# A YOCO step on one core: page scores in eight groups of two pages, six key pages ahead, the bias table later, key rows finished by ScalarE

## The chip, the cores and the metric

The kernel runs on one core of one Trainium2 chip. The metric is the device time of one execution in microseconds (us), from runs of the same program on the same chip; fewer is better.

## The reference

One inference step of a hybrid decoder with D = 1024 for 256 prompt tokens and 8 x 8 sample tokens (320 rows). Layer one is retention (4 heads, chunks of 128). Then one shared K/V is made from the residual stream, and layer two is block-sparse attention (8 heads of 128) that reads it. Each of the 8 sample sequences also has 2 pages of 128 old positions in a paged cache. The part that matters here:

```python
kv = rmsnorm(x, kv_norm_w) @ w_kv
k, v = jnp.split(kv, 2, axis=-1)
k = rmsnorm(k.reshape(B, T, MOBA_HEADS, MOBA_HD), k_norm_w)
...
k_past = cache_k[pages].reshape(past, MOBA_HEADS, MOBA_HD)
...
s_own = jnp.einsum('qhd,qlhd->qhl', q, k_own).astype(jnp.float32) + b_own
...
p = jax.nn.softmax(logits, axis=-1)
```

For the sample tokens all 256 old positions and the own ones are scored, with a bias by distance.

## The kernel before

The kernel is written as one program per engine, all of which walk the same list of steps, made by hand in `make_schedule` (L133 to L294). The large work is the projections: weights come in chunks of 1 MB (SyncE, `load_chunk`, L648), ScalarE rounds them to a high part (`w_hi`, L1208), VectorE makes the rest (`w_lo`, L1537), and TensorE (PE) multiplies high by high, high by low and low by high into a PSUM bank per tile (L888, L904, L907, in `project`, L847). A chunk of the key projection (`mk`) has three tiles: two of 12 matmuls, one of 8. Each tile has a place in its middle and one at its end, the gaps, into which `make_schedule` puts other steps. The lists `g` count these gaps: 0 to 5 lie in chunk mk(0,0), 6 to 11 in mk(0,1), 12 to 17 in mk(1,0), 18 to 23 in mk(1,1), 24 to 29 in the first chunk of the value projection. The stage from 331.6 to 405.7 us of the profiled run is these five chunks; "key stage" means it.

The steps in these gaps:

- `KP n`, VectorE: turns page n of old keys (L1829) from a cache slot into `ktc` or a part of `scr` (`ktc2`), 128 x 1024. 16 pages; SyncE loads page n + 3 at KP n, with four DMAs, into one of NCP = 4 slots, once page n - 1 has been turned (`load_page`, L682).
- `KS q`, PE: plain fp32 scores of the sample queries (spread out in `wide`) against four turned pages: 64 matmuls of 32x32 by 256 columns (L1079), each shown as two records. KS 0 and 1 add up in PSUM banks 3 to 6 (`PS_BANKS`), KS 2 and 3 again. KP n waits for the group that read its place before.
- `SE 0` and `SE 1`, VectorE: take these banks out, with the bias (L1842, four operations).
- `KX c`, PE: transposes finished key rows into banks 6 and 7 (L1095); VectorE and ScalarE copy them to `mkT` (L1832, L1469).
- A tile of `mk`: ScalarE squares it (L1376), VectorE sums per head (L1697), ScalarE takes the root (L1378), VectorE the reciprocal (L1700) and then four multiplies of 128x128, each by the row's factor and by `k_norm_w` (`knw`) (L1706), into `rows`. SyncE stores `rows` to the outputs k_out at KX 0 and KX 2 (L812). The first multiply of the second half of the keys waits until the first half has been stored (`rows_stored`).
- At KP 10 SyncE also issues the bias table `tb` of 1 MB (L806). `SN`, `SA`, `SD` and `SB` are the scores against the own rows and the softmax. From L1138 on `PV` multiplies with the pages of old values, which use the same cache slots (pages 16 to 31 in `load_page`).

Within an engine steps run strictly in order, and SyncE's DMA issues too: an issue that waits holds all behind it.

## Time and profile before

| | us |
|---|---|
| median of 3 runs | 518.03 (517.72 to 518.62) |
| the profiled execution | 518.44 |
| its span | 516.7 |
| PE busy in it | 495.1 |
| VectorE busy | 362.6 |
| ScalarE busy | 252.2 |

A row of instructions in the profile gives the line, the engine, the operation, what it writes and reads, how many there are, the busy time and the mean time in ns of one, and then the idle time before them and what ended it. PEld is the load of weights into the array, DVE is VectorE, ACT is ScalarE, SPq is SyncE's queue. PEclk, the granted clock, is 1.00 at 2.4 GHz and 0.50 at 1.2 GHz. "issue" is a wait for nothing that the profile shows. The stages before 331 us are the retention layer and the query projection, those after 405 us the values, the attention and the output.

### The profile page before, as it was taken

The page shows a single profiled execution, that of the slowest core. Times are in us where ns is not written, and L with a number is a line of the kernel's source. Part 1 is how long each engine was busy: PE and PEld are TensorE (multiplying, and loading weights), DVE is VectorE, ACT ScalarE, POOL GpSimd, SP SyncE. Part 2 cuts the span into 40 slices and gives each one's busy share as a digit, 9 for nine tenths or more (in the row PEclk, how much of TensorE's full clock was granted, in tenths as well). Part 3 has the DMA queues.
Part 4 walks back from the last instruction along what each step waited for, and adds up shares of the span by engine and source line. Part 5 has one row for each costly group of instructions (what it writes and reads, how often), then busy time and mean ns, then how long its engine had stood idle before and what let it go on. Part 6 is the DMA issues. An engine that isn't in the chain of part 4 may idle for free.

```text
span 516.7 us, 9892 instructions
## 1 busy us (share of the span) xinstructions
PE 495.1 (96%) x3689; PEld 427.3 (83%) x3689; DVE 362.6 (70%) x655; ACT 252.2 (49%) x508; POOL 87.9 (17%) x123
## 2 busy tenths in 40 slices
PE   8999999999999999999999999996776999999997
PEld 6989977898779977897999999874555878999885
DVE  3865449882989549891898888868647664776662
ACT  6736631773436641672734547733113655555540
POOL 0381005320082004520000144410000000000000
PEclk9999999999999999999999999997978999999999
DMA  9992959999799989999659989369888437785211
GB/s 272 357 348 84 297 224 352 376 330 270 271 358 324 220 239 335 387 284 219 203 168 317 314 218 255 100 206 253 242 209 257 163 121 244 236 308 175 82 51 51
DMA packets 86291, 125.53 MB, mean 243 GB/s; under 512 B 4820, under 2 KB 51109, under 8 KB 86117
## 3 DMA queue, kind: packets, MB, share of 16 engines
q1 hardware_dynamic: 86162, 124.90, 78.2%
q8 instruction: 29, 0.48, 0.4%
q14 instruction: 18, 0.14, 0.1%
q10 hardware_dynamic: 82, 0.02, 0.0%
HBM read 98.93 MB, written 27.57 MB: 245 GB/s over the span
## 4 chain that ended last, share of the span: by engine, by line
PE 69%; DVE 16%; DMA 7%; issue 3%; ACT 2%; SPq 2%; POOL 0%; DVEq 0%; ACTq 0%; POOLq 0%
PE bank L907 34%; PE bank L904 15%; PE bank L888 5%; DVE w_lo L1537 5%; DMA w_raw<-in_ret_w_in 3%; DMA w_raw<-in_ret_w_out 3%; DVE st L1759 3%; PE bank L1079 2%; PE bank L1138 2%; DVE scr L1829 1%; PE bank L1016 1%; DVE ktc L1829 1%; PE bank L1184 1%; DMA v_rows<-vs_split 1%; DVE scr L1795 1%
## 5 line engine op out<-in xcount | busy, mean ns | idle before, releaser
L1537 DVE TENSOR_TENSOR w_lo<-w_raw,w_hi 128x512 fp32r<-128x512 f32 x207 | 144.4, 736 | 63.5 <-ACT w_hi L1208 62.9
L1208 ACT ACTIVATE w_hi<-w_raw 128x512 fp32r<-128x512 f32 x208 | 118.7, 621 | 61.9 <-PE bank L907 33.6
L907 PE MATMUL bank<-xn_hi,w_hi 128*128 128x320 f32 x320 | 100.2, 317 | 0.9 <-ACT w_hi L1208 0.7
L907 PE MATMUL bank<-xn_hi,w_lo 128*128 128x320 f32 x320 | 97.7, 309 | 0.1
L907 PE MATMUL bank<-xn_lo,w_hi 128*128 128x320 f32 x320 | 97.6, 309 | 0.0
L904 PE MATMUL bank<-w_hi,xn_hi 128*128 128x512 f32 x160 | 65.7, 411 | 0.0
L907 PEld LDWEIGHTS bank<-xn_hi,w_hi 128*128 128x128 f32 x320 | 59.7, 188 | 5.3 <-issue 3.6
L904 PE MATMUL bank<-w_hi,xn_lo 128*128 128x512 f32 x160 | 63.0, 394 | 0.0
L904 PE MATMUL bank<-w_lo,xn_hi 128*128 128x512 f32 x160 | 63.0, 394 | 0.0
L907 PE MATMUL bank<-ym_hi,w_hi 128*128 128x320 f32 x192 | 60.9, 317 | 0.0
L907 PEld LDWEIGHTS bank<-xn_lo,w_hi 128*128 128x128 f32 x320 | 59.8, 188 | 0.4 <-DVE xn_lo L1586 0.2
L907 PEld LDWEIGHTS bank<-xn_hi,w_lo 128*128 128x128 f32 x320 | 59.7, 188 | 0.3 <-DVE w_lo L1537 0.3
L907 PE MATMUL bank<-ym_hi,w_lo 128*128 128x320 f32 x192 | 59.3, 309 | 0.0
L907 PE MATMUL bank<-ym_lo,w_hi 128*128 128x320 f32 x192 | 59.3, 309 | 0.0
L1759 DVE SCALAR_TENSOR_TENSOR st<-st,bank 128x512 f32<-128x512 f32 x64 | 39.6, 682 | 5.2 <-PE bank L1030 5.2
L904 PEld LDWEIGHTS bank<-w_hi,xn_hi 128*128 128x128 f32 x160 | 30.5, 191 | 9.7 <-issue 3.7
L907 PEld LDWEIGHTS bank<-ym_hi,w_hi 128*128 128x128 f32 x192 | 36.1, 188 | 1.8 <-issue 1.7
L907 PEld LDWEIGHTS bank<-ym_lo,w_hi 128*128 128x128 f32 x192 | 36.1, 188 | 0.1
L1969 POOL TENSOR_TENSOR fin<-raw_qk,cst 128x320 f32<-128x320 f32 x16 | 17.4, 1108 | 109.9 <-DMA out_ret_state_prompt<-fin 68.7
L904 PEld LDWEIGHTS bank<-w_lo,xn_hi 128*128 128x128 f32 x160 | 30.5, 190 | 6.8
L907 PEld LDWEIGHTS bank<-ym_hi,w_lo 128*128 128x128 f32 x192 | 36.0, 188 | 0.0
L904 PEld LDWEIGHTS bank<-w_hi,xn_lo 128*128 128x128 f32 x160 | 30.7, 192 | 5.6
(280 smaller groups left out, 776.6 us busy)
## 6 DMA issues: line engine op xcount, KB each, us to landing
w_raw<-in_ret_w_in SPq DMA_DIRECT2D x23, 1024.0 KB, 10.8
st<-in_state_ret SPq DMA_DIRECT2D x32, 512.0 KB, 8.9
out_ret_state_sample<-st SPq DMA_DIRECT2D x32, 512.0 KB, 4.6
w_raw<-in_ret_w_out SPq DMA_DIRECT2D x8, 1024.0 KB, 8.7
w_raw<-in_moba_w_in SPq DMA_DIRECT2D x8, 1024.0 KB, 6.5
cache<-in_cache_k SPq DMA_DIRECT2D x64, 128.0 KB, 4.6
w_raw<-in_w_kv SPq DMA_DIRECT2D x8, 1024.0 KB, 7.7
cache<-in_cache_v SPq DMA_DIRECT2D x16, 512.0 KB, 4.4
```

The source lines that it names most:

```text
L888: mm = pe.matmul(bank[b][:, :], xn_hi[:, k, TP:T + TS], w[:, wk, :], start=k == 0 and n == 0, stop=k == KT - 1 and n == 1)
L904: mm = pe.matmul(bank[b][0:m, :], x[:, k, c0:c0 + m], w[:, wk, :], **flags)
L907: mm = pe.matmul(bank[out][:, 0:T], w[:, wk, P * tile:P * tile + P], x[:, k, :], **flags)
L1016: mm = pe.matmul(bank[5][32 * j:32 * j + 32, :], qz[:, q0:q0 + 32], st[:, b, DV * d:DV * d + DV], start=False, stop=g == 1 and d == 1, ski ...
L1079: last[g] = pe.matmul(bank[PS_BANKS[g]][c0:c0 + 32, 0:PAST], wide[rows_at, 8 * h + 2 * e + q // 2, at:at + 32], keys_of, start=q % 2 == 0 ...
L1138: mm = pe.matmul(bank[7][32 * j:32 * j + 32, P * u:P * u + P], window(8 * half_at + 4 * (j // 2) + 2 * pg + j % 2, b % 4), cache[:, (16 + ...
L1184: pe.matmul(bank[6][:, 0:TP], mvp[:, 0, P * h:P * h + P], pt[:, h % 2, 0:TP], start=True, stop=False)
L1208: act.activation(w_hi[:, c % 2, part], w_raw[:, c % RAW, part], ACT.Copy).then_inc(w_hi_done, 1)
L1537: dve.tensor_tensor(w_lo[:, c % 2, part], w_raw[:, c % RAW, part], w_hi[:, c % 2, part].bitcast(F32), ALU.subtract).then_inc(w_lo_done, 1)
L1759: dve.scalar_tensor_tensor(state, state, math.exp(NEW * LOG_DECAY[h]), bank[up_bank(b, d)][:, :], ALU.mult, ALU.add).then_inc(bank_read[up ...
L1829: dve.transpose(keys_turned(n), cache[:, n % NCP, :].rearrange("p (c x j) -> p x c j", c=4, j=32)).then_inc(kt_done, 1)
L1969: done(pool.tensor_tensor(to, x, tab, ALU.mult))
```

## The change

Four edits:

1. **Groups of two pages.** KS has eight groups u of two pages instead of four of four, each of 64 matmuls of 32x32 by 128 columns; the total of columns stays. Groups 0 to 3 fill the banks, then 4 to 7. They stand at gaps 4, 7, 10, 13, 17, 19, 22 and 25, and the transposes of pages 2u+4 and 2u+5 one gap behind group u. KP 0 and 1 move into the last two tiles of the query projection, KP 2 and 3 to gaps 0 and 1. Pages are taken in another order, so that `ktc` and `ktc2` each hold one page of a pair. SE 0 moves from gap 12 to 14, SE 1 from 24 to 26, KX 0 from 14 to 15; KX 1, 2 and 3 stay at 16, 26 and 27.
2. **Six pages ahead.** Pages 4 and 5 go to `early_pages`, the still unused memory of `mkT`, so SyncE loads page n + 5 at KP n. The copies to `mkT` wait until these pages are turned. The residual is kept in cache slots 2, 3 and 0.
3. **The bias table** is issued by SyncE at group 6, behind value pages 1 and 2, instead of at KP 10.
4. **Key rows.** VectorE multiplies the whole tile by `knw` in one operation (new L1734) and takes the reciprocal; a new step `KN` on ScalarE scales the four heads (new L1497), at gaps 8, 10, 12, 20, 22 and 24. Its semaphore `rows_done` is what the stores of k_out and KX wait for.

```diff
@@ -47,7 +47,7 @@
 CW = 2048
 RAW = 3
 NST = 8
-NCP = 4
+NCP, NSLOT = 4, 6
 FAR = PAST + NEW - 1
 LINE = 392
 TOK = [(0, P), (P, P), (TP, TS)]
@@ -111,8 +111,18 @@
 
 def key_page(n):
 
-    q, s, pg = n // 4, n % 4 // 2, n % 2
+    q, pg, s = n // 4, n // 2 % 2, n % 2
     return NPG * (4 * (q // 2) + 2 * s + q % 2) + pg
+
+
+def page_slot(n):
+
+    return n if n < NSLOT else (n - 2) % NCP
+
+
+def page_count(n):
+
+    return sum(64 if m < 16 else 16 for m in range(n + 1) if page_slot(m) == page_slot(n))
 
 
 def sb_bank(pair):
@@ -248,14 +260,18 @@
     g[0].append(("ME", 7))
     g[3] += [("QS", 1), ("QR",)]
     g[5].append(("QT",))
-    for n, at in enumerate((0, 1, 2, 3, 6, 7, 8, 9, 12, 13, 14, 15, 18, 19, 20, 21)):
-        g[at].append(("KP", n))
-    for q, at in enumerate((5, 11, 17, 23)):
-        g[at].append(("KS", q))
-    g[12].append(("SE", 0))
-    g[24].append(("SE", 1))
-    g[14].append(("KX", 0))
+    g[0].append(("KP", 2))
+    g[1].append(("KP", 3))
+    for u, at in enumerate((4, 7, 10, 13, 17, 19, 22, 25)):
+        g[at].append(("KS", u))
+        if u < 6:
+            g[at + 1] += [("KP", 2 * u + 4), ("KP", 2 * u + 5)]
+    g[14].append(("SE", 0))
+    g[26].append(("SE", 1))
+    g[15].append(("KX", 0))
     g[16].append(("KX", 1))
+    for n, at in enumerate((8, 10, 12, 20, 22, 24)):
+        g[at].append(("KN", n))
     g[26].append(("KX", 2))
     g[27].append(("KX", 3))
     g[28] += [("SN",), ("SA", 0), ("SA", 1)]
@@ -536,16 +554,20 @@
 
         def keys_turned(n):
 
-            at = ktc if n % 4 < 2 else ktc2
-            return at[:, n % 2, :, :]
+            return (ktc, ktc2)[n % 2][:, n // 2 % 2, :, :]
+
+        def page_at(n):
...
@@ -682,19 +704,20 @@
             def load_page(n):
 
                 m, vals = (n - 16, True) if n >= 16 else (key_page(n), False)
-                if n >= 16 + NCP:
-                    sp.wait_ge(pv_done, n - 15 - NCP)
-                elif n >= NCP:
-                    sp.wait_ge(kt_done, n - NCP + 1)
+                before = n - (NCP if n >= NCP + NSLOT else NSLOT)
+                if before >= 16:
+                    sp.wait_ge(pv_done, before - 15)
+                elif before >= 0:
+                    sp.wait_ge(kt_done, before + 1)
                 page = sp.value_load(pages[0:1, m:m + 1], min_val=0, max_val=a["cache_k"].shape[0] - 1)
                 if vals:
-                    sp.dma_start(cache[:, n % NCP, :], a["cache_v"][bass.ds(page, 1)].rearrange("o p h d -> p (o h d)"))\
-                        .then_inc(cache_loaded[n % NCP], 16)
+                    sp.dma_start(page_at(n), a["cache_v"][bass.ds(page, 1)].rearrange("o p h d -> p (o h d)"))\
+                        .then_inc(cache_loaded[page_slot(n)], 16)
                     return
                 src = a["cache_k"][bass.ds(page, 1)].rearrange("o (c i) h d -> i (o c) (h d)", i=32)
                 for g in range(4):
-                    sp.dma_start(cache[32 * g:32 * g + 32, n % NCP, :].rearrange("p (c x) -> p c x", c=4), src[:, :, 256 * g:256 * g + 256])\
-                        .then_inc(cache_loaded[n % NCP], 16)
+                    sp.dma_start(page_at(n)[32 * g:32 * g + 32, :].rearrange("p (c x) -> p c x", c=4), src[:, :, 256 * g:256 * g + 256])\
+                        .then_inc(cache_loaded[page_slot(n)], 16)
 
             to, src = chunk_view(w_raw, 0, 0), chunk_source(0)
             sp.dma_start(st[:, 0, :], x_rows[0]).then_inc(x_loaded[0], 16)
@@ -783,13 +806,14 @@
                 elif kind == "US":
                     store_pair(4 * step[1] + 3)
                     load_pair(4 * step[1] + 6)
-                elif kind == "ME" and 1 <= step[1] <= NCP:
+                elif kind == "ME" and 1 <= step[1] <= NSLOT and step[1] != 5:
                     if step[1] == 1:
                         sp.wait_ge(pages_loaded, 16)
                         await_ret_over(sp)
                         sp.dma_start(knw[:, :], bass.AP(a["k_norm_w"].tensor, 0, [[0, P], [1, HD]])).then_inc(knw_loaded, 16)
                     load_page(step[1] - 1)
                 elif kind == "ME" and step[1] == 5:
+                    load_page(4)
                     sp.wait_ge(lines_stored, 64)
                     for h in range(MH):
                         for s in range(2):
@@ -799,16 +823,16 @@
                                 .then_inc(bias_loaded, 16)
                 elif kind == "KP":
                     n = step[1]
-                    if n:
-                        load_page(n + 3)
-                    if n == 10:
-                        await_full(sp, 5, "QSS")
-                        sp.dma_start(tb[:, :, :], bass.AP(scratch.tensor, FAR - P, [[skew, P], [LINE, MH], [1, TP]]))\
-                            .then_inc(tb_loaded, 16)
+                    if 1 <= n <= 13:
+                        load_page(n + NSLOT - 1)
+                elif kind == "KS" and step[1] == 6:
+                    await_full(sp, 5, "QSS")
+                    sp.dma_start(tb[:, :, :], bass.AP(scratch.tensor, FAR - P, [[skew, P], [LINE, MH], [1, TP]]))\
+                        .then_inc(tb_loaded, 16)
                 elif kind == "KX" and step[1] % 2 == 0:
                     p = step[1] // 2
                     for t, (c0, m) in enumerate(TOK):
-                        await_read(sp, *tile_use("mk", 3 * p + t))
+                        sp.wait_ge(rows_done, 3 * p + t + 1)
                         sp.dma_start(k_out[t][:, 512 * p:512 * p + 512], rows[0:m, t, :]).then_inc(rows_stored, 16)
                 elif kind == "SN":
                     load_page(16 + NCP - 1)
@@ -1062,12 +1086,13 @@
                         mm = pe.transpose(bank[7][:, P * t:P * t + P], q_rows[:, P * t:P * t + P], ident)
                     close(mm, 7)
                 elif kind == "KS":
-                    q = step[1]
-                    pe.wait_ge(kt_done, 4 * q + 4)
+                    u = step[1]
+                    q, pg = u // 2, u % 2
+                    pe.wait_ge(kt_done, 2 * u + 2)
                     pe.wait_ge(wide_filled, MH)
-                    if q % 2 == 0:
+                    if u % 4 == 0:
                         for b in PS_BANKS:
-                            await_free(pe, b, "PS", q // 2)
+                            await_free(pe, b, "PS", u // 4)
                     last = {}
                     for e in range(4):
                         for s in range(2):
@@ -1075,19 +1100,19 @@
                             for h in range(2):
                                 for g in range(4):
                                     rows_at, c0 = slice(32 * g, 32 * g + 32), 32 * (2 * h + s)
-                                    keys_of = (ktc, ktc2)[s][rows_at, :, 4 * h + e, :]
-                                    last[g] = pe.matmul(bank[PS_BANKS[g]][c0:c0 + 32, 0:PAST], wide[rows_at, 8 * h + 2 * e + q // 2, at:at + 32],
-                                                        keys_of, start=q % 2 == 0 and e == 0, stop=q % 2 == 1 and e == 3,
+                                    keys_of = (ktc, ktc2)[s][rows_at, pg, 4 * h + e, :]
+                                    last[g] = pe.matmul(bank[PS_BANKS[g]][c0:c0 + 32, P * pg:P * pg + P],
+                                                        wide[rows_at, 8 * h + 2 * e + q // 2, at:at + 32], keys_of,
+                                                        start=u % 4 == 0 and e == 0, stop=u % 4 == 3 and e == 3,
                                                         skip_group_check=True)
-                    if q % 2:
+                    if u % 4 == 3:
                         for g in range(4):
                             close(last[g], PS_BANKS[g])
                     else:
                         last[3].then_inc(ks_done, 1)
                 elif kind == "KX":
                     c = step[1]
-                    for t in range(3):
-                        await_read(pe, *tile_use("mk", 3 * (c // 2) + t))
+                    pe.wait_ge(rows_done, 3 * (c // 2) + 3)
                     def key_columns(i, t):
 
                         c0 = TOK[t][0]
@@ -1464,7 +1489,16 @@
                     ins = act.activation(rsq[:, 16:20], bank[7][:, TP:TP + P].rearrange("p (j m) -> p j m", m=32)[:, :, 0],
                                          ACT.Sqrt, bias=eps[:, 1:2])
                     ins.then_inc(bank_read[7], 1)
+                elif kind == "KN":
+                    n = step[1]
+                    m = TOK[n % 3][1]
+                    await_read(act, *tile_use("mk", n))
+                    for d in range(4):
+                        ins = act.activation(rows[0:m, n % 3, P * d:P * d + P], rows[0:m, n % 3, P * d:P * d + P], ACT.Copy,
+                                             scale=kss[0:m, n % 2, d:d + 1])
+                    ins.then_inc(rows_done, 1)
                 elif kind == "KX":
+                    act.wait_ge(kt_done, NSLOT)
                     await_full(act, 7, *step)
                     act.activation(mkT[:, 2 * step[1] + 1, :], bank[7][:, 0:T], ACT.Copy).then_inc(bank_read[7], 1)
                 elif kind == "SA":
@@ -1687,25 +1721,22 @@
                         m = TOK[i][1]
                         if nk == 0:
                             dve.wait_ge(knw_loaded, 16)
-                        src = bank[b]
                         if i == 2:
-                            src = rows[:, i, :]
                             upper_half(rows[0:TS, i, :], b).then_inc(sum_done, 1)
                         dve.wait_ge(key_sq_done, nk + 1)
                         if nk >= 2:
-                            await_read(dve, *tile_use("mk", nk - 2))
+                            dve.wait_ge(rows_done, nk - 1)
                         dve.tensor_reduce(kss[0:m, nk % 2, :], key_sq[0:m, :].rearrange("p (h d) -> p h d", d=HD), AX.X, ALU.add)\
                             .then_inc(key_sum_done, 1)
-                        dve.wait_ge(kss_done, nk + 1)
-                        done(dve.reciprocal(kss[0:m, nk % 2, :], kss[0:m, nk % 2, :]))
-                        done.wait()
                         if h:
                             dve.wait_ge(rows_stored, 48)
                             await_full(dve, 7, "KX", 1)
-                        for d in range(4):
-                            ins = dve.scalar_tensor_tensor(rows[0:m, i, P * d:P * d + P], src[0:m, P * d:P * d + P],
-                                                           kss[0:m, nk % 2, d:d + 1], knw[0:m, :], ALU.mult, ALU.mult)
-                        ins.then_inc(bank_read[b], 1)
+                        done(dve.tensor_tensor(rows[0:m, i, :].rearrange("p (h d) -> p h d", d=HD),
+                                               (rows[0:m, i, :] if i == 2 else bank[b][:, :]).rearrange("p (h d) -> p h d", d=HD),
+                                               knw[0:m, :].rearrange("p (o d) -> p o d", o=1).broadcast_to((m, 4, HD)), ALU.mult))
+                        done.wait()
+                        dve.wait_ge(kss_done, nk + 1)
+                        dve.reciprocal(kss[0:m, nk % 2, :], kss[0:m, nk % 2, :]).then_inc(bank_read[b], 1)
                         nk += 1
                     elif what == "mo" and i == 2:
                         await_read(dve, xr_bank(4 + h), "XR", 4 + h)
@@ -1823,10 +1854,10 @@
                     done.wait()
                 elif kind == "KP":
                     n = step[1]
-                    dve.wait_ge(cache_loaded[n % NCP], page_loaded(n))
+                    await_page(dve, n)
                     if n >= 4:
-                        await_ks(dve, n // 4 - 1)
-                    dve.transpose(keys_turned(n), cache[:, n % NCP, :].rearrange("p (c x j) -> p x c j", c=4, j=32)).then_inc(kt_done, 1)
+                        await_ks(dve, n // 2 - 2)
+                    dve.transpose(keys_turned(n), page_at(n).rearrange("p (c x j) -> p x c j", c=4, j=32)).then_inc(kt_done, 1)
                 elif kind == "KX":
                     await_full(dve, 6, *step)
                     dve.tensor_copy(mkT[:, 2 * step[1], :], bank[6][:, 0:T]).then_inc(bank_read[6], 1)
```

VectorE around SE 0, before. `scr` and `ktc` are what the transposes (L1829) write; L1842 is SE 0.

```order
L1537 TENSOR_TENSOR w_lo<-w_raw,w_hi 128x512 [waits w_hi_done] x2
L1829 STREAM_TRANSPOSE ktc<-cache 128x1024 [waits bank_full6,cache_loaded0]
L1842 SCALAR_TENSOR_TENSOR ps<-bank,small,bs 128x256 [waits bank_full5,bank_full4,bank_full6,bank_full3,bias_loaded]
L1842 SCALAR_TENSOR_TENSOR ps<-bank,small,bs 128x256
L1842 SCALAR_TENSOR_TENSOR ps<-bank,small,ps 128x256 [waits bank_read5,bank_read3]
...
L1829 STREAM_TRANSPOSE ktc<-cache 128x1024 [waits bank_full6,cache_loaded1]
L1537 TENSOR_TENSOR w_lo<-w_raw,w_hi 128x512 [waits w_hi_done]
L1829 STREAM_TRANSPOSE scr<-cache 128x1024 [waits bank_full6,cache_loaded2]
L1832 COPY mkT<-bank 128x320 [waits bank_full6]
```

The same place after the change, where L1860 is the transpose, L1873 SE 0, L1571 the `w_lo` split and L1863 the copy of KX:

```order
L1571 TENSOR_TENSOR w_lo<-w_raw,w_hi 128x512 [waits w_hi_done] x3
L1860 STREAM_TRANSPOSE ktc<-cache 128x1024 [waits bank_full6,cache_loaded0]
L1860 STREAM_TRANSPOSE scr<-cache 128x1024 [waits bank_full6,cache_loaded1]
L1873 SCALAR_TENSOR_TENSOR ps<-bank,small,bs 128x256 [waits bank_full5,bank_full4,bank_full6,bank_full3,bias_loaded]
L1873 SCALAR_TENSOR_TENSOR ps<-bank,small,bs 128x256
L1873 SCALAR_TENSOR_TENSOR ps<-bank,small,ps 128x256 [waits bank_read5,bank_read3]
...
L1863 COPY mkT<-bank 128x320 [waits bank_full6]
```

Two transposes (KP 10 and 11) and three splits now stand ahead of SE 0, where one transpose and two splits stood, and no transpose is left between SE 0 and the copy.

SyncE at the stores of the first half of the keys, before (L806 is the bias table, L689 and L696 the next page of keys):

```order
L806 DMA tb<-bias_lines 128x8x256 [waits bank_full5]
L812 DMA out_k_prompt<-rows 128x512 [waits bank_read2]
L812 DMA out_k_prompt<-rows 128x512 [waits bank_read0]
L812 DMA out_k_sample<-rows 64x512 [waits bank_read1]
L689 TENSOR_LOAD pages [waits kt_done]
```

and after (L712 and L714 load a page of values, L677 a weight chunk, L836 are the stores, L830 the table):

```order
L712 TENSOR_LOAD pages [waits kt_done]
L712 ISA x2
L714 ISA
L714 DMA cache<-in_cache_v 128x1024
L836 DMA out_k_prompt<-rows 128x512 [waits rows_done] x2
L836 DMA out_k_sample<-rows 64x512 [waits rows_done]
L677 DMA w_raw<-in_w_kv 128x4x512 [waits w_lo_done]
...
L830 DMA tb<-bias_lines 128x8x256 [waits bank_full5]
```

The stores now stand behind the first page of values, whose load waits until page 12 of the keys has been turned (KP 12, gap 18), and the table is behind both.

## Rows read from the trace of the kernel before

**Rows 1.** The page: busy time of each engine, and PE in 40 slices.

```profile
PE 495.1 (96%) x3689; PEld 427.3 (83%) x3689; DVE 362.6 (70%) x655; ACT 252.2 (49%) x508; POOL 87.9 (17%) x123
...
PE   8999999999999999999999999996776999999997
```

**Rows 2.** Windows: length, busy of PE, PEld, DVE, ACT, POOL, PEclk, DMA share, GB/s.

```profile
320.00:330.00 10.00, 10.00 (x73) 9.39 (x72) 9.25 (x18) 8.79 (x23) 3.91 (x12) 1.00 0.35 116
...
350.00:360.00 10.00, 5.04 (x132) 2.84 (x130) 8.50 (x19) 3.90 (x8) 0.00 (x0) 0.68 1.12 234
...
370.00:380.00 10.00, 5.42 (x104) 3.42 (x101) 2.38 (x3) 0.33 (x1) 0.00 (x0) 0.71 1.04 308
380.00:390.00 10.00, 6.66 (x28) 5.13 (x26) 6.40 (x15) 3.32 (x7) 0.00 (x0) 0.95 0.71 167
390.00:400.00 10.00, 8.46 (x149) 6.27 (x150) 8.11 (x18) 2.60 (x6) 1.04 (x2) 0.83 0.87 276
```

**Rows 3.** Waits of PE in the key stage, 331 to 406 us.

```profile
PE bank L1079 <- DVE scr L1829: 9.8, 2, 5.0
PE bank L1079 <- issue: 4.6, 1, 4.6
```

**Rows 4.** The same windows view for three groups of scores, L1079 alone.

```profile
340.30:343.00 2.70, 2.70 (x128) 1.79 (x128) 1.00 0.78 205
355.50:360.00 4.50, 4.50 (x128) 2.66 (x128) 0.50 1.10 257
391.50:395.60 4.10, 4.06 (x128) 2.61 (x128) 0.62 0.94 297
```

**Rows 5.** Chain of waits, 320 to 410 us: start, us, what.

```profile
377.59 4.56 PE bank L904 x12
```

**Rows 6.** Timeline of PE before the first key transposes (L1095).

```profile
363.70 0.39 PE L904 MATMUL bank<-w_hi,xn_hi 128*128 128x512 f32 x1
...
364.39 0.38 PE L1095 MATMUL bank<-eye,rows 128*128 128x128 f32 x2
```

**Rows 7.** Timeline of VectorE between score groups 0 and 1.

```profile
353.15 1.13 DVE L1706 SCALAR_TENSOR_TENSOR rows<-bank,small,knw 128x128 f32<-128x128 f32 x4
354.19 1.24 DVE L1829 STREAM_TRANSPOSE scr<-cache 128x1024 f32<-128x1024 f32 x1
```

**Rows 8.** Groups of VectorE instructions, 331 to 406 us.

```profile
L1829 DVE STREAM_TRANSPOSE scr<-cache 128x1024 f32<-128x1024 f32 x8 | 9.8, 1230 | 0.0
L1563 DVE TENSOR_TENSOR rows<-bank,rows 64x512 f32<-64x512 f32 x2 | 1.3, 672 | 0.0
L1842 DVE SCALAR_TENSOR_TENSOR ps<-bank,small,ps 128x256 f32<-128x256 f32 x2 | 0.9, 480 | 0.1
L1537 DVE TENSOR_TENSOR w_lo<-w_raw,w_hi 128x512 fp32r<-128x512 f32 x20 | 13.1, 674 | 2.0 <-ACT w_hi L1208 2.0
```

**Rows 9.** Forms of L1115, then L1138 (ns min/median/max, first and last start); group 0's.

```profile
L1115 PE MATMUL bank<-mkT,mvp x64: 219/219/243, 403.5 to 404.4; 128*32 128x64 f32 x64
...
L1138 PE MATMUL bank<-cache,wide x256: 272/273/298, 415.7 to 474.4; 128*32 128x128 f32 x128
...
L1079 PE MATMUL bank<-scr,wide 32*32 32x256 f32 x64 | 2.6, 385 | 0.0
```

**Rows 10.** Timeline of SyncE's issues around the bias table.

```profile
367.54 0.42 SPq L806 DMA_DIRECT2D tb<-bias_lines  x1
368.02 1.14 SPq L812 DMA_DIRECT2D out_k_prompt<-rows  x2
369.20 0.74 SPq L812 DMA_DIRECT2D out_k_sample<-rows  x1
```

**Rows 11.** Groups of ScalarE instructions, 331 to 406 us.

```profile
L1269 ACT ACTIVATE tb<-ps 128x256 f32<-128x256 f32 x1 | 0.4, 401 | 0.0
```

**Rows 12.** Issues from 364 to 378 us: KB each, median us to landing.

```profile
tb<-bias_lines SPq DMA_DIRECT2D x1, 1024.0 KB, 6.8
...
out_k_sample<-rows SPq DMA_DIRECT2D x1, 128.0 KB, 8.3
```

34 lines of the change are left out of this document (20 added, 14 removed), and 2 rows, old and new, of the table banks.

## The prediction

> **What bounds the kernel now.** First the page: TensorE (PE) is busy 495.1 us, 96% of the span, and apart from the last slice the digits under 8 stand in slices 28 to 31 alone [rows 1], 349 to 400 us at 12.9 us a slice. So all but some 20 us of this kernel is PE work, and a change pays only in that stage. The windows say which stage: PE is busy 5.04, 5.42, 6.66 and 8.46 of 10 us in four of the windows from 350 us on, at a granted clock of 0.68, 0.71, 0.95 and 0.83; from 320 to 330 us it is full [rows 2]. That is the key projection with the page scores in it. Then its waits: 9.8 us in two waits of the score matmuls (L1079) on VectorE's transposes (L1829), and 4.6 us once on "issue" [rows 3]. The windows of the score groups give the clock's part: the first group takes 2.70 us at 1.00 (2.4 GHz), the two behind the waits 4.50 us at 0.50 (1.2 GHz) and 4.10 us at 0.62 [rows 4]. Last the chain: behind the "issue" wait, 12 projection matmuls take 4.56 us [rows 5]. At full clock three of them start in 0.69 us [rows 6], so 12 take 2.76. The stage loses 9.8 + 4.6 us in waits, 1.8 + 1.4 us of slow score groups and 1.8 us of slow projection.
>
> **Why PE waits there.** VectorE can turn pages 4 to 7 only when group 0 has read pages 0 to 3, and it does so between the pieces of two key tiles: the last transpose starts at 354.19 us, behind a reduce, a reciprocal and 1.13 us of multiplies [rows 7]. Group 1 needs all four.
>
> **The change, part by part.** The sum goes by the profiled run, 518.44 us.
>
> 1. *Groups of two pages, the transposes of group u+2 right behind group u.* A group now needs pages that were due a whole group earlier: between u and u+2 lie 5 or 6 half tiles, each 6 x 0.23 = 1.38 us or 0.9 us, against 2 x 1.23 us of transposes [rows 8]. Both waits go: -9.8 us, and the slow clock behind them: -3.2 us. The first transposes move into the query projection, where VectorE is busy 9.25 of 10 us but PE is never idle [rows 2]; I cost that at nothing, since its cover is weights split well ahead; without it, it is 2.5 us.
>
> 2. *Eight groups of 64 matmuls of 128 columns for four of 64 of 256.* No row shows this form. Before, 4 x 2.7 = 10.8 us at full clock. Upper end: the time of an instruction stays, 8 x 2.70 = 21.6, +10.8 us. Lower end: time goes with columns, 1.35 us a group, no change in all (a gain is excluded: the same columns pass). The nearest rows: 64 records of a 64-column form start within 0.9 us, about 15 ns apart, and the 128-column form lasts 273 ns where the scores' last 385 [rows 9]; records of the scores stand 2.70/128 = 21 ns apart [rows 4]. In these rows time falls with columns, so I take 1.4 us a group, 11.2 us: +0.4 us. The Trainium skill ("TensorEngine Tiling (Array Packing)", Instruction Overhead) gives each matmul an overhead of some 60 cycles, and says that fewer columns than that bring nothing; by it the 128 columns still pay, and an estimate from the page for 64 instructions at 25 ns is 1.6 us a group, +2 us in all. The same page (Key Properties) says that a change of tiling mode drains the engine, which would count against twice as many groups; in the rows PE goes into the first group without idle time [rows 4].
>
> 3. *A new wait at the first key transposes (KX 0).* They write bank 6, which SE 0 must have read, and the bank is complete only with group 3. Before, two gaps and 4.4 us lay between group 1's end and KX 0 (360.0 [rows 4] to 364.39 [rows 6]). Now group 3 stands at gap 13, KX 0 at gap 15: 2 x 1.38 = 2.8 us of PE work. VectorE has to do two transposes (2.4) and SE 0 (1.8: four of 0.45 to 0.48 [rows 8]) first, 4.2 us and some 0.3 us to start: a wait of 1.7 us, and of 3.7 us if the three weight splits ahead of them (0.67 each [rows 8]) have not been done. For KX 2, behind group 7 at gap 25 with one half tile between: 1.8 + 0.3 - 1.4 = 0.7 us, or 2.7 us with the splits. Together 2.4 to 6.4; I take +4 us, near the middle, because the splits follow the weights' arrival.
>
> 4. *k_out behind the first V page.* SyncE must wait for transpose 12 before it issues V page 0, and the three k_out stores are queued behind that; the last lands 8.3 us after issue [rows 12]. Before, they were issued at 368.0 to 369.9 us [rows 10], early. VectorE's first multiply of the second half of the keys waits for them. Transpose 12 ends some 1.4 us after group 4, the stores have landed some 10 us later (0.4 + 1.1 + 0.7 us of issuing [rows 10], then 8.3), and VectorE would be ready 5 us after group 4 (0.9 + 2.8 of PE, 1.3 of square and reduce): it stands some 6 us. Behind it are transposes 14, 15, two tiles, splits and SE 1. PE has 10.9 us of projection and two groups until group 7, so most of it is covered; what is left is 0 to 3.5 us at group 7 and KX 2. I take +2 us.
>
> 5. *Keys: one multiply and four ScalarE steps.* VectorE saves 1.13 us for one operation of about 0.68 us (the 64x512 row of L1563 [rows 8]), 6 times, 2.7 us in all, off PE's path but for part 3, where it is in. ScalarE gets 24 activations of 128x128, each at most the 0.40 us of 128x256 [rows 11], under 10 us, and is idle 6 of 10 us there [rows 2]: nothing. KX needs them, but they are issued one to three gaps ahead.
>
> 6. *The bias table later, six pages ahead.* The 1 MB issued at 367.54 us, just ahead of the "issue" stall [rows 10], moves behind group 6, and two pages come into the stretch from 320 us, where the DMA share is 0.35 [rows 2]. Its first reader stands four gaps into the next chunk but one, over 10 us later, and the landing takes 6.8 us [rows 12]. Nothing on the path by itself. Whether the stall goes with it is a rival: PE's stream now holds 256 more matmuls, and the stall (4.6 + 1.8 us) stays in my forecast once.
>
> 7. *The clock behind the new waits.* 6 us of new waits stand for 9.8 of old ones, which cost 3.2 us of slow clock; in proportion +2 us.
>
> Sum: 518.44 - 9.8 - 3.2 + 0.4 + 4 + 2 + 2 = 513.8. The median of before is 0.4 us under its profiled run: **513.4 us**.
>
> **The rivals.**
> - *The stall goes too.* For: the DMA engines stood at a share of 1.04 in that window, just after the table and the k_out stores were issued, and the stall is one of a kind. Against: more instructions in the same time. 513.4 - 4.6 - 1.8 = 507.0. Chance 0.17.
> - *Small matmuls cost what the big ones did.* Against: rows 9. +10.4: 523.8, slower. It decides from 2.1 us a group on (519.1). Chance 0.06.
> - *A second instruction stall, the slower side.* The stream of PE in the groups is twice as long, in a stretch in which the DMA shares are 0.7 to 1.1 [rows 2]; one more stall of the same price, 6.4 us with its clock, gives 519.8. It decides from 5.7 us on, that is with one whole stall. Chance 0.13.
> - *The new waits take the old ones' place.* Parts 3 and 4 at their upper ends, 6.4 + 3.5, and the whole 3.2 us of clock: 518.4 - 9.8 + 0.4 + 9.9 = 518.9, less 0.4: 518.5, no change. It needs weights that arrive late. Chance 0.13.
> - *Pages late.* The shares were near 1 where the pages were fetched [rows 2]; in a shorter stage the DMA engines may set the pace. 1 to 6 us over the forecast. Chance 0.04.
>
> The forecast itself has 0.47. About 0.2% is what a measurement of this kernel can tell, 517.0 to 519.1. Faster: 0.45 of the forecast, 0.17 and 0.11 of the rest, 0.73. Same 0.10, slower 0.17. The range reaches down to 506.5, which holds the first rival and the lower ends of parts 2 to 4, and up to 519.5, so that the fourth is in, and the second and about half of the third are out.
>
> **What would show it.** No wait of the score matmuls on L1860 (the new number of the transposes) over 0.5 us; groups of 1.1 to 1.6 us; PE waits of 1 to 4 us at the key transposes with VectorE's SE or ScalarE's rows named; VectorE standing some 6 us before the fourth multiply of keys; one "issue" stall. Wrong it is if the groups last over 2 us, if "issue" has over 6 us in the stage, or if PE still waits over 9 us there in all.

## The result and the profile after

| | before | after |
|---|---|---|
| median of 4 runs, us | 518.21 (517.72 to 518.62) | 524.79 (523.28 to 526.29) |
| the profiled execution, us | 518.44 | 526.29 |
| its span | 516.7 | 524.5 |
| PE busy | 495.1 | 500.4 |

The change makes the kernel slower: the ratio is 1.0126, with a 95% interval of 1.0099 to 1.0154. The forecast was 513.4 us, faster with a chance of 0.73; the measured time lies above the range, which ends at 519.5. The profiled run of the changed kernel is the slowest of its four, so a second profile of the same kernel (run e14 below, there the fastest of four) stands beside it where the two differ.

The key stage (the same five chunks) now runs from 331.7 to 413.6 us, 81.9 us for 74.1 before. The page of the kernel after, PE and clock in 40 slices, to hold against [rows 1]:

```profile
PE 500.4 (95%) x4201; PEld 433.0 (83%) x4201; DVE 360.0 (69%) x637; ACT 259.3 (49%) x532; POOL 87.7 (17%) x123
...
PE   8999999999999999999999999996487999999997
...
PEclk9999999999999999999999999999689899999999
```

Waits of PE in the kernel after, 300 to 425 us (engine, line, what ended them: us in total, times, longest). They answer to [rows 3]; L1104 are the scores, L1120 is KX, L1873 is SE.

```profile
PE bank L1120 <- DVE ps L1873: 10.6, 1, 10.6
PE bank L1120 <- DVE scr L1873: 3.6, 1, 3.6
PE bank L1104 <- issue: 3.3, 3, 2.7
```

The two waits of 5 us on the transposes are gone, as meant. In their place PE stands 10.6 us at KX 0 and 3.6 us at KX 2, both times until VectorE has taken the scores out of bank 6. Windows of the kernel after, of the score matmuls alone (columns as in [rows 4]):

```profile
339.16:341.00 1.84, 1.84 (x128) 1.52 (x128) 1.00 0.90 347
...
351.74:353.57 1.83, 1.83 (x128) 1.53 (x128) 1.00 0.04 9
...
398.93:400.76 1.83, 1.83 (x128) 1.52 (x128) 1.00 1.04 320
```

A group of 128 columns takes 1.83 us at full clock, and does so whether the DMA engines are idle (0.04) or full (1.04). Half the columns cost 68% of the 2.70 us in [rows 4], not half.

What held SE 0 is read upwards. Timelines of VectorE, ScalarE and SyncE in the kernel after, each with its engine (in brackets the idle time before and what ended it):

```profile
365.84 1.29 DVE L1571 TENSOR_TENSOR w_lo<-w_raw,w_hi 128x512 fp32r<-128x512 f32 x2 [4.29 <-ACT w_hi L1233]
368.05 0.69 DVE L1571 TENSOR_TENSOR w_lo<-w_raw,w_hi 128x512 fp32r<-128x512 f32 x1 [0.92 <-ACT w_hi L1233]
368.66 1.24 DVE L1860 STREAM_TRANSPOSE ktc<-cache 128x1024 f32<-128x1024 f32 x1
369.82 1.20 DVE L1860 STREAM_TRANSPOSE scr<-cache 128x1024 f32<-128x1024 f32 x1
370.95 0.83 DVE L1873 SCALAR_TENSOR_TENSOR ps<-bank,small,bs 128x256 f32<-128x256 f32 x2
```

```profile
365.18 1.15 ACT L1233 ACTIVATE w_hi<-w_raw 128x512 fp32r<-128x512 f32 x2 [6.38 <-DMA w_raw<-in_w_kv]
```

```profile
336.84 0.40 SPq L677 DMA_DIRECT2D w_raw<-in_w_kv  x1
338.03 17.53 SPq L719 DMA_DIRECT2D cache<-in_cache_k  x16
355.66 0.40 SPq L677 DMA_DIRECT2D w_raw<-in_w_kv  x1
356.84 8.87 SPq L719 DMA_DIRECT2D cache<-in_cache_k  x12
```

Ahead of SE 0 stand the splits of the weights of mk(1,1), those wait for ScalarE, and ScalarE stood 6.38 us for the chunk itself, which SyncE issued at 355.66 us, behind four pages that took it from 338.03 on. The chain of waits names the rest: page 10, the last of the four, waits for its slot until the transpose of page 6 at 350.70, and only then is the chunk issued.

```profile
350.70 1.25 DVE ktc L1860
...
355.66 9.49 DMA w_raw<-in_w_kv
365.18 1.15 ACT w_hi L1233 x2
```

In the kernel before, the same chunk was issued at 344.12 us, 11.5 us earlier, and landed 5.6 us later:

```profile
344.12 0.40 SPq L655 DMA_DIRECT2D w_raw<-in_w_kv  x1
```

The step KP n loads page n + 5, but from page 10 on there are only four slots: page 10 is asked for at gap 5 and can be issued only after the transpose at gap 8, while the chunk's load comes at gap 6, behind it.

KX 2 has a second wait behind it: VectorE's first multiply of the second half of the keys stood 2.7 us for the k_out stores (4.4 us in e14), which now come behind value page 0.

```profile
DVE rows L1734 <- DMA out_k_sample<-rows: 2.7, 1, 2.7
```

**The ledger** of the two profiled runs, which are 7.85 us apart: the waits on transposes -9.8; KX 0 and KX 2 +14.2; issue -1.3 (4.6 to 3.3); eight groups for four at full clock, 14.7 for 10.8, +3.9. The slow clock costs what it did, in other places: in the chain of the kernel after, KX 0 takes 1.51 us where KX 1 takes 0.68, four matmuls behind it 1.71 where four take 0.92 later, 12 matmuls from 382.5 us on some 4.5 for 2.76, and 1.7 us around KX 2 (6 matmuls 2.51 for 1.38); about 5 us in all, for 3.2 + 1.8 before. That is +7.0; some 0.8 us remain that I have put nowhere.

### The profile page after: what moved, and what is told of

It reads as the page before. It is cut to its first block, busy times and chain, and to the rows that moved or that the text cites. A ratio compares the mean times of both kernels' runs of the same rounds, so it can differ in the third digit from the quotient of the medians.

```text
span 524.5 us, 10931 instructions
## 1 busy us (share of the span) xinstructions
PE 500.4 (95%) x4201; PEld 433.0 (83%) x4201; DVE 360.0 (69%) x637; ACT 259.3 (49%) x532; POOL 87.7 (17%) x123
## 4 chain that ended last, share of the span: by engine, by line
PE 77%; DMA 9%; DVE 6%; ACT 3%; issue 3%; SPq 1%; POOL 0%; DVEq 0%; ACTq 0%; POOLq 0%
PE bank L931 39%; PE bank L928 16%; PE bank L912 6%; DMA w_raw<-in_w_kv 4%; DMA w_raw<-in_ret_w_out 3%; PE bank L1040 2%; PE bank L1163 2%; ACT w_hi L1233 1%; PE bank L1054 1%; DVE w_lo L1571 1%; DVE ktc L1860 1%; DMA v_rows<-vs_split 1%; PE bank L987 1%; DMA out_k_sample<-rows 1%; PE bank L1209 1%
## 5 line engine op out<-in xcount | busy, mean ns | idle before, releaser
L1571 DVE TENSOR_TENSOR w_lo<-w_raw,w_hi 128x512 fp32r<-128x512 f32 x207 | 144.6, 737 | 73.1 <-ACT w_hi L1233 72.3
```

The lines of the kernel that those rows point to most:

```text
L1571: dve.tensor_tensor(w_lo[:, c % 2, part], w_raw[:, c % RAW, part], w_hi[:, c % 2, part].bitcast(F32), ALU.subtract).then_inc(w_lo_done, 1)
```

## The experiments

Each is against the kernel before, timed beside it, whose medians were 518.0 to 518.5 us (a single 519.17 beside e13). The single runs of the kernel before lie between 514.7 and 522.2 us, so differences of about 1 us between two experiments mean nothing. Waits come from one profiled run each, and e14 shows how far two profiles of one kernel can differ.

**e1: pages in time.** From the changed kernel:

```diff
-                    if 1 <= n <= 13:
-                        load_page(n + NSLOT - 1)
+                    if 1 <= n <= 4:
+                        load_page(n + NSLOT - 1)
+                    elif n >= 7:
+                        load_page(n + NCP - 1)
```

> The changed kernel, but SyncE issues key page 10 and the later pages only at KP n-3, when their slot is free or nearly so, instead of at KP n-5; pages 4 to 9 as in the change. Theory W (weights held back: SyncE stands for a slot with page 10, and the weight chunk of mk(1,1) queued behind it is issued at 355.66 us and lands at 365.18, so the splits ahead of SE 0 and with them KX 0 wait 10.6 us): the chunk is issued by 348 us, the wait at KX 0 falls to under 3.5 us, the slow clock behind it goes, the k_out stores come before the first value page, and the time is 512 to 517 us. Rival V (VectorE's row of two transposes, three splits and SE 0 is itself the wait): KX 0 still waits 5 us or more, time 519 to 523. Rival G (the eight groups are the loss): over 521 whatever the weights do.

Measured: 519.0 us, ratio 1.0022 (0.9986 to 1.0057): the loss against before is gone, though the time is above the 512 to 517 expected. ScalarE waits 1.49 us, for an earlier chunk, and no longer for this one (issued at 349.88). The edit moves a second thing: value page 0 is now loaded behind the k_out stores, and VectorE no longer waits for them. Waits of PE in e1:

```profile
PE bank L1106 <- issue: 4.4, 3, 3.2
PE bank L1122 <- DVE ps L1875: 4.2, 1, 4.2
PE bank L1122 <- DVE scr L1875: 1.5, 1, 1.5
```

W and V are both true in part: of the wait at KX 0, 4.2 us are VectorE's own row, and what was above that was the late chunk. The time fell by the chunk and the stores together; e2 and e3 take them apart.

**e2: weights first.** From the changed kernel; the stores stay where they are.

```diff
+EARLY = {4: ("mk", 0, 1), 8: ("mk", 1, 0), 11: ("mk", 1, 1)}
...
-                    load_chunk(c + 2)
+                    if chunks[c] not in EARLY.values():
+                        load_chunk(c + 2)
...
+                    if n in EARLY:
+                        load_chunk(chunks.index(EARLY[n]) + 2)
                     if 1 <= n <= 13:
                         load_page(n + NSLOT - 1)
```

> The changed kernel with nothing moved but three weight chunks of w_kv on SyncE: each is issued just ahead of the page that would wait for its slot (pages 9, 13 and 16). The k_out stores stay behind the first value page. W: nearly all of the gain of the run before it, 513 to 518 us, with a wait of up to 3 us of VectorE's L1734 for the stores left. If the stores behind the value page are what costs: 521 us or more. Rival V: 519 to 523 with 5 us or more at KX 0.

Measured: 525.56 us, ratio 1.0129 (1.0056 to 1.0202), a miss. The chunk was issued at 341.92 us and KX 0 waited 4.2 us, the same as in e1, so the mechanism holds; but PE stood 8.1 us on issue. Waits of PE in e2:

```profile
PE bank L1108 <- issue: 8.1, 3, 5.4
PE bank L1124 <- DVE ps L1877: 4.2, 1, 4.2
PE bank L1124 <- DVE scr L1877: 2.9, 1, 2.9
```

So no run shows the early chunk alone to save time: what was won at KX 0 was lost in waits on issue. That wait had been one row of my forecast; e4, e5, e10, e13 and e15 look at it.

**e3: stores first.** From the changed kernel: page 16 is loaded behind the k_out stores of KX 0 and not at KP 11.

```diff
-                    if 1 <= n <= 13:
+                    if 1 <= n <= 13 and n != 11:
                         load_page(n + NSLOT - 1)
...
                         sp.dma_start(k_out[t][:, 512 * p:512 * p + 512], rows[0:m, t, :]).then_inc(rows_stored, 16)
+                    if p == 0:
+                        load_page(16)
```

> The changed kernel with nothing moved but the first value page on SyncE, from ahead of the k_out stores to behind them; the weight chunks stay late. W: VectorE's 2.7 us wait for the stores goes, PE's 10.6 us at KX 0 stay, time 522 to 525 us. If the stores are the main loss: under 520 us.

Measured: 522.17 us, ratio 1.0079 (1.0044 to 1.0113), within the expectation. VectorE's wait for the stores, 2.7 us in the profile after, is gone. But KX 0 waited only 4.9 us, though this edit lies behind it: the chunk was issued at 352.68 us there. So part of the 10.6 us belonged to the one profiled run; see e14. Waits of PE in e3:

```profile
PE bank L1106 <- issue: 6.5, 4, 4.6
PE bank L1122 <- DVE ps L1875: 4.9, 1, 4.9
PE bank L1122 <- DVE scr L1875: 1.0, 1, 1.0
```

The wait at KX 2 is 1.0 us, where the change has 3.6 and 4.5. Over all variants it follows VectorE's wait for the stores: 1.0 to 1.7 us at KX 2 where VectorE waits for none (e1, e3, e9), 2.9 where it waits 1.4 and 2.2 us (e2, e15), 3.6 and 4.5 where it waits 2.7 and 4.4. So the stores behind the value page did cost PE some 2 to 3.5 us at KX 2; e3's time does not show it, because its waits on issue are 3 to 5 us longer than those of the two profiles of the change.

**e4: the late table alone.** From the kernel before: the issue of `tb` moves from KP 10 to KS 3.

```diff
-                    if n == 10:
-                        await_full(sp, 5, "QSS")
-                        sp.dma_start(tb[:, :, :], bass.AP(scratch.tensor, FAR - P, [[skew, P], [LINE, MH], [1, TP]]))\
-                            .then_inc(tb_loaded, 16)
+                elif kind == "KS" and step[1] == 3:
+                    await_full(sp, 5, "QSS")
+                    sp.dma_start(tb[:, :, :], bass.AP(scratch.tensor, FAR - P, [[skew, P], [LINE, MH], [1, TP]]))\
+                        .then_inc(tb_loaded, 16)
```

> The kernel before with one part of the change alone: the 1 MB bias table is issued at KS 3 instead of KP 10. If the table's transfer starved PE of instructions, the 4.6 us of issue in KS 2 and the slow clock behind it go: 512 to 515 us. If it did not (the changed kernel has a stall of 2.7 us in the scores with no table near): 517 to 519 us and a stall of 2 us or more in one of the groups.

Measured: 514.65 us, ratio 0.9932 (0.9907 to 0.9957). The wait at the same place fell from 4.58 us [rows 3] to 1.8; the transposes' 9.8 stayed. Waits of PE in e4:

```profile
PE bank L1079 <- DVE scr L1829: 9.8, 2, 5.0
PE bank L1079 <- issue: 1.8, 1, 1.8
```

**e5: the groups split, alone.** From the kernel before: each group of four pages becomes two halves, back to back.

```diff
+                    for pg, e in [(pg, e) for pg in range(2) for e in range(4)]:
...
-                                    keys_of = (ktc, ktc2)[s][rows_at, :, 4 * h + e, :]
-                                    last[g] = pe.matmul(bank[PS_BANKS[g]][c0:c0 + 32, 0:PAST], wide[rows_at, 8 * h + 2 * e + q // 2, at:at + 32],
+                                    keys_of = (ktc, ktc2)[s][rows_at, pg, 4 * h + e, :]
+                                    last[g] = pe.matmul(bank[PS_BANKS[g]][c0:c0 + 32, P * pg:P * pg + P],
+                                                        wide[rows_at, 8 * h + 2 * e + q // 2, at:at + 32],
```

> The kernel before with one part of the change alone: each score group of four pages is issued as two halves of two pages, 64 matmuls of 128 columns each, back to back in the same gap; nothing is moved. In the changed kernel a group of 128 columns takes 1.84 us at full clock where 256 columns took 2.70. Theory G: PE gets 8 x 1.84 - 4 x 2.70 = +3.9 us, less where the clock is low, and at least as much stall on issue as before (4.6 us), for 256 more matmuls: 520 to 525 us. Rival: columns decide, 4 x 2.7 stays and nothing changes, 517 to 519 us.

Measured: 536.60 us, ratio 1.0364 (1.0335 to 1.0394), 18 us slower, far past both theories. Waits of PE in e5:

```profile
PE bank L1079 <- issue: 15.7, 5, 5.5
PE bank L1079 <- DVE scr L1830: 9.8, 2, 5.0
```

and its timeline at the third group (start, length, ..., in brackets the idle time before):

```profile
380.04 0.34 PE L1079 MATMUL bank<-scr,wide 32*32 32x128 f32 x8 [4.04 <-issue]
387.88 0.68 PE L1079 MATMUL bank<-scr,wide 32*32 32x128 f32 x16 [5.48 <-issue]
```

That PE runs out of instructions here, with 128 short matmuls in a row, is so far a reading of the word "issue"; the traces are asked below. The page counts 33 transfers of instructions (0.54 MB) for 29 (0.48 MB) before, as in the changed kernel. That one has as many short matmuls, but two to four half tiles of projection between two groups, and its two profiles have 3.3 and 1.8 us of issue, its variants e1, e2, e3, e9 and e15 between 4.4 and 8.1.

**e10 and e13: is it the transfers?** From e5, with data left out: in e10 of key pages 4 to 15 only 8 of 256 columns of each piece are loaded, so these scores are of old data; in e13 also only 8 of 1024 columns of the value pages and 8 of 256 columns of one head of the bias table, so the attention's output is of old data.

```diff
+                w = 256 if n < NCP else 8
...
-                    sp.dma_start(cache[32 * g:32 * g + 32, n % NCP, :].rearrange("p (c x) -> p c x", c=4), src[:, :, 256 * g:256 * g + 256])\
+                    sp.dma_start(cache[32 * g:32 * g + 32, n % NCP, :].rearrange("p (c x) -> p c x", c=4)[:, :, 0:w], src[:, :, 256 * g:256 * g + w])\
```

```diff
-                    sp.dma_start(cache[:, n % NCP, :], a["cache_v"][bass.ds(page, 1)].rearrange("o p h d -> p (o h d)"))\
+                    sp.dma_start(cache[:, n % NCP, 0:8], a["cache_v"][bass.ds(page, 1)].rearrange("o p h d -> p (o h d)")[:, 0:8])\
...
-                        sp.dma_start(tb[:, :, :], bass.AP(scratch.tensor, FAR - P, [[skew, P], [LINE, MH], [1, TP]]))\
+                        sp.dma_start(tb[:, 0:1, 0:8], bass.AP(scratch.tensor, FAR - P, [[skew, P], [LINE, 1], [1, 8]]))\
```

> The run e5 (each group split in halves) with the transfers taken away: of key pages 4 to 15 only 8 of 256 columns of each row piece are loaded, so their scores are of old data; number of DMAs, instructions and waits as in e5. e5 has 15.7 us of issue in the groups. Theory I (PE runs out of instructions because their fetch, 16 KB a piece, stands in DMA queues filled by the pages): with the pages gone the issue waits fall under 6 us, time 520 to 528 us, while the two waits of 5 us on VectorE's transposes stay. Rival: the stall is of the split matmuls themselves or of their number, whatever the DMA engines do: issue stays above 12 us and the time at 534 to 538 us.

> The run e10 with the transfers taken away that were left in the stage beside the weights: of the value pages 8 of 1024 columns, of the bias table 8 of 256 columns of one head, so the attention's output is of old data. In e10 no issue wait fell into the 20 us from 350 us on, where the DMA share was 0.10 and 0.38, and 4.9 + 1.8 us beside the table and weights, 3.2 us beside the value pages. Theory I (the fetch of PE's instructions queues behind transfers): the 4.9 us wait falls under 2 us, the one of 3.2 us too, and issue is under 5 us in all; time 522 to 527 us. Rival (the number of matmuls in a row sets the stall): 9 to 12 us of issue again, at the same places, and 530 us or more.

Measured, in one run each: 531.87 and 524.87 us. Waits of PE in e10, then in e13:

```profile
PE bank L1080 <- issue: 11.1, 4, 4.9
```

```profile
PE bank L1080 <- issue: 8.5, 4, 2.7
```

Neither theory is right alone. The waits fall with the transfers, 15.7, 11.1, 8.5 us, and the longest from 5.5 to 2.7; but four waits of 1.7 to 2.7 us stay, two of them in stretches with a DMA share of 0.06, one at 0.32 and one, of 1.83 us, at 0.93 beside a weight chunk. In e10 the wait of 4.88 us lay at a share of 1.02; the wait at the same place in e13 took 2.69 us at 0.06. Window of e10 (columns as in [rows 2]):

```profile
374.00:379.00 5.00, 0.33 (x16) 0.06 (x6) 0.57 (x1) 0.00 (x0) 0.00 (x0) 1.00 1.02 293
```

**What the traces show of these waits.** The traces hold the transfers of instructions too, in pieces of 16 KB on a queue of their own, q8. It has 29 pieces before and 33 after, 4 more for 512 more matmul records and as many weight loads, so they are PE's. In the kernel before, the wait of 4.58 us lies from 371.90 to 376.48 us. The view of the DMA queues has no piece from 372 to 373 us, and this for 373 to 374 us:

```profile
q8 instruction: 1, 0.02, 6.6%
```

That is one piece, busy for 6.6% of 16 engines' 1 us, or 1.05 us; it starts at 373.94 us and lands at 374.99. PE goes on 1.49 us later. Some of the others, all times in us:

| run | PE waits from, to | piece starts, lands | PE goes on after landing |
|---|---|---|---|
| before | 371.90, 376.48 | 373.94, 374.99 | 1.49 |
| after | 379.43, 382.10 | 379.50, 380.73 | 1.37 |
| e4 | 371.17, 373.01 | 370.26, 371.57 | 1.44 |
| e5, the longest | 382.40, 387.88 | 385.07, 386.37 | 1.51 |
| e13, the longest | 372.43, 375.12 | 372.37, 373.71 | 1.41 |
| e15, the longest | 374.76, 380.84 | 378.05, 379.47 | 1.37 |

In the 16 profiles there are 28 waits on issue of 0.9 us or more between 330 and 430 us. Every one of them ends 1.2 to 1.7 us after a piece has landed, and that piece took 0.9 to 1.5 us. So PE did run out of instructions in them, and a wait that begins with the start of its piece lasts 2 to 3 us. The rest is the late start of the piece: in 11 of the 28 it starts 0.7 to 3.3 us after the wait has begun, and the DMA share up to that start is then 0.76 to 1.13. In e5 these late starts add up to 5.1 us, in e10 to 3.5, in e13 to nothing. A full share does not always bring one: in the profile after it was 1.03 in the 2 us ahead of a piece that started with the wait. Which transfer a late piece stood behind, and when PE asked for it, no view shows.

**e6: the key rows alone.** From the kernel before, with KN at the start of gaps 8, 10, 12, 20, 22 and 24:

```diff
-                        dve.wait_ge(kss_done, nk + 1)
-                        done(dve.reciprocal(kss[0:m, nk % 2, :], kss[0:m, nk % 2, :]))
...
-                        for d in range(4):
-                            ins = dve.scalar_tensor_tensor(rows[0:m, i, P * d:P * d + P], src[0:m, P * d:P * d + P],
-                                                           kss[0:m, nk % 2, d:d + 1], knw[0:m, :], ALU.mult, ALU.mult)
+                        done(dve.tensor_tensor(rows[0:m, i, :].rearrange("p (h d) -> p h d", d=HD),
+                                               (rows[0:m, i, :] if i == 2 else bank[b][:, :]).rearrange("p (h d) -> p h d", d=HD),
+                                               knw[0:m, :].rearrange("p (o d) -> p o d", o=1).broadcast_to((m, 4, HD)), ALU.mult))
+                        done.wait()
+                        dve.wait_ge(kss_done, nk + 1)
+                        dve.reciprocal(kss[0:m, nk % 2, :], kss[0:m, nk % 2, :]).then_inc(bank_read[b], 1)
```

> The kernel before with one part of the change alone: key rows multiplied by knw on VectorE in one operation and scaled by ScalarE in a new step. VectorE saves 1.13 - 0.68 = 0.45 us a tile; two tiles lie ahead of the last transpose of groups 1 and 3, and the root no longer stands in front of the multiply (0.36 us each), so each of the two 5 us waits falls by 1 to 1.5 us: 515 to 518 us. Rival: KX now waits for ScalarE instead, 518 to 520 us.

Measured: 515.19 us, ratio 0.9934 (0.9912 to 0.9956). The waits of groups 1 and 3 fell from 9.8 to 6.3 us, and the wait on issue from 4.6 to 2.4, though the table was not touched. Waits of PE in e6:

```profile
PE bank L1082 <- DVE scr L1836: 6.3, 2, 3.2
PE bank L1082 <- DVE mkT L1839: 2.6, 1, 2.6
PE bank L1082 <- issue: 2.4, 1, 2.4
PE bank L1097 <- DVE ps L1849: 1.0, 1, 1.0
```

Part of it comes back as new waits, 2.6 us for a copy of KX that frees bank 6 and 1.0 us at KX 0. The four kinds of wait add up to 12.3 us for 14.4, so 2.2 us of what this one profile gained is the wait on issue (its piece of instructions started 0.2 us ahead of the wait, before 2.0 us behind its beginning) and not VectorE's row.

**e8: turn together.** From e4:

```diff
-    for n, at in enumerate((0, 1, 2, 3, 6, 7, 8, 9, 12, 13, 14, 15, 18, 19, 20, 21)):
+    for n, at in enumerate((0, 1, 2, 3, 6, 6, 6, 6, 12, 13, 14, 15, 18, 18, 18, 18)):
```

> The kernel before with the bias table late (as in e4) and the four transposes of a group together at gaps 6 and 18, directly behind the group that frees their places, instead of one at each of four gaps between the key tiles; groups of four pages stay. If VectorE's order made the two waits of 5 us, and not the pages' arrival: waits under 2 us each, no slow clock, 506 to 511 us. If the pages' transfers are late in any case: the waits stay above 3 us and the time is 513 to 516 us.

Measured: 521.16 us, ratio 1.0058 (1.0038 to 1.0078), 6.5 us slower than e4. Waits of VectorE in e8, then of PE:

```profile
DVE scr L1829 <- DMA cache<-in_cache_k: 8.6, 3, 4.4
```

```profile
PE bank L1095 <- DVE ps L1842: 5.5, 1, 5.5
PE bank L1095 <- DVE scr L1842: 4.4, 1, 4.4
PE bank L1079 <- DVE scr L1829: 2.8, 1, 2.8
```

One score wait went and the other fell to 2.8 us, but now VectorE itself stood 8.6 us for pages, in order, with key tiles and splits behind, and PE met that at KX. It is the changed kernel's trap in another form.

**e9: SE 0 first.** From e1: `g[14].insert(0, ("SE", 0))` for `g[14].append(("SE", 0))`.

> The run e1 (pages in time) with SE 0 moved ahead of the transposes of pages 10 and 11 on VectorE, same gap. What is left of the wait at KX 0 in e1 is 4.2 us. If it is VectorE's row (two transposes of 1.2 us ahead of SE 0): it falls by 2.4 us to under 2 us and the time by 2 to 4 us, to 515 to 517 us. If the three splits behind their weights are all of it: no change, 518 to 520 us.

Measured: 517.52 us, ratio 0.9969 (0.9938 to 1.0000). The wait at KX 0 fell from 4.2 to 2.0 us and 0.9 us came at KX 1. The time is 1.5 us under e1's, with intervals that overlap, so it is the wait that shows the part of the two transposes:

```profile
PE bank L1106 <- issue: 5.0, 3, 4.3
PE bank L1122 <- DVE ps L1875: 2.0, 1, 2.0
```

**e11 and e12: the two parts that gain.** e11 is e4 and e6 together; e12 is e11 with KP 5 and KP 13 at gaps 6 and 18.

```diff
-    for n, at in enumerate((0, 1, 2, 3, 6, 7, 8, 9, 12, 13, 14, 15, 18, 19, 20, 21)):
+    for n, at in enumerate((0, 1, 2, 3, 6, 6, 8, 9, 12, 13, 14, 15, 18, 18, 20, 21)):
```

> The kernel before with two parts of the change and no other: the bias table late (e4, -3.9 us) and the key rows finished by ScalarE (e6, -3.4 us). If they act on different waits (issue; transposes) they add up: 510 to 513 us. If both act on the same stretch: 513 to 516 us.

> The run e11 with one transpose of each group of four (pages 5 and 13) moved one gap forward, beside the one before it, where VectorE stood idle for 2.3 us. If it is VectorE's order that holds groups 1 and 3, their waits of 3.2 us fall by about 1.2 us each: 1 to 3 us faster than e11. If the pages' arrival holds them (e8 waited 8.6 us for pages): as e11 within 1 us.

Measured: e11 512.78 us, ratio 0.9907 (0.9873 to 0.9940); e12 512.40 us, ratio 0.9883 (0.9839 to 0.9928). Of 3.9 + 3.4 us that the parts gained alone, 5.2 are left together (against 517.99 beside them). 512.78 lies inside the range for different waits, but its interval, 511.4 to 514.9, reaches well into the other, so the two theories are not told apart. The waits speak for an overlap: both parts had shortened the same wait on issue, to 1.8 us in e4 and 2.4 in e6, and together it is 2.7. e12 is not to be told from e11; its waits on the transposes fell from 6.7 to 5.1 us, but VectorE now waited 3.4 us for pages, where it had waited 2.2. Both beat the kernel before and the changed one.

**e14 and e15: the change again, and with its table early.** e14 is the changed kernel. e15 is it with the issue of `tb` back in KP 10, behind that step's page.

> The changed kernel itself, profiled and timed again. If the wait of 10.6 us at KX 0 is the rule: a wait of 8 us or more, the weight chunk issued at 355 us or later, time 523 to 526 us. If it belongs to the slowest run: a wait of 4 to 7 us, the chunk issued about 352.7 us as in e3, ScalarE waiting under 3 us for it, and a time of 520 to 524 us.

> The changed kernel with one part undone: the bias table is issued at KP 10 again, ahead of the k_out stores. Before the change, moving it away gained 3.9 us, by a stall on issue that fell from 4.6 to 1.8 us. If PE's instructions stand behind that 1 MB here too: 2 to 5 us slower than e14, 524 to 529 us, with more than 5 us of issue. If in the changed order it meets nothing: as e14 within 1 us.

Measured: e14 522.35 us (521.74 to 528.08), ratio 1.0108 (1.0044 to 1.0171); e15 525.10 us, ratio 1.0142 (1.0071 to 1.0213). Waits of PE in e14, then in e15:

```profile
PE bank L1120 <- DVE ps L1873: 6.3, 1, 6.3
PE bank L1120 <- DVE scr L1873: 4.5, 1, 4.5
PE bank L1104 <- issue: 1.8, 3, 1.1
```

```profile
PE bank L1104 <- issue: 7.0, 3, 6.1
PE bank L1120 <- DVE ps L1873: 5.9, 1, 5.9
```

In e14 the chunk was issued at 353.37 us and ScalarE waited 2.98 us for it. Two profiles of this kernel have 10.6 and 6.3 us at KX 0, and e3, with the same order up to there, has 4.9. What differs between the first two is how long two weight chunks took to land: the one issued at 336.8 us 9.8 us in the first and 7.5 in e14, the late one 9.5 and 7.4. The first holds the split ahead of transpose 6 (350.70 and 349.08 us), which frees page 10's slot, and so the issue of the second; together they make ScalarE's start 4.4 us later, 365.18 for 360.82. By these differences some 4.2 of the 10.6 us are VectorE's row (e1, e2), 4.3 go with the slow transfers of that one run, and 2.1 with the order of SyncE, which in e3 cost only 0.7. The slow transfers count because the order leaves no time for them: in e1 the same chunk took 10.1 us to land, and ScalarE did not wait for it.

With the table early the longest issue wait is 6.1 us where it was 1.1. But e2 and e3 have waits of 5.4 and 4.6 us with the table late, so that in the changed kernel it is not shown to be the table and no other transfer. The medians differ by 2.75 us, the way expected, and their intervals overlap.

## Why the prediction was wrong

By the steps of the prediction:

1. **The old waits** (-9.8, -3.2): right, both are gone and all eight groups run at 1.00. The first transposes in the query projection cost nothing, PE is full there.
2. **Eight groups** (+0.4, bounds 0 to +10.8): mis-sized. 1.83 us a group, not 1.40, is +3.9 us. The value lies inside the bounds; I took it near the lower one because two other forms got cheaper with columns, and these were forms with fewer, wider tiles. The estimate of +2 us from the Trainium skill ("TensorEngine Tiling (Array Packing)", Instruction Overhead, some 60 cycles a matmul) was nearer: 1.6 us a group for 1.83 measured. [rows 4] begins with the group and so can't show idle time ahead of it; the window from 336 to 346 us, which holds the first group, has PE busy for all of its 10.00 us.
3. **KX 0 and KX 2** (2.4 to 6.4, taken +4): the place and the engine were right, the size was not: 14.2 us, and 10.8 in e14. This is the step that failed, in the sentence "the splits follow the weights' arrival": I let the three splits cost at most their own length and never asked when their weights were issued. The row of [rows 10] shows SyncE in order, and in part 4 I followed what value page 0 holds up; I did not do the same for page 10, which waits for transpose 6 at gap 8 and holds the chunk of gap 6. At KX 0 the sum had 1.7 to 3.7 us; the runs show 10.6, 6.3 and 4.9 with the order of the change, and 4.2 where the chunk comes in time (e1, e2). e9 shows that 2.2 of these 4.2 are the two transposes ahead of SE 0, which the sum had (2.4). At KX 2 it had 0.7 to 2.7: 1.0 to 1.7 are measured where nothing waits for the stores, and the rest up to 3.6 and 4.5 belongs to part 4.
4. **k_out behind the value page** (+2): VectorE stood 2.7 us, and 4.4 in e14, not 6. The price was about right all the same: some 2 to 3.5 us at KX 2 go with it (e3). The time of e3, 522.17 us for e14's 522.35, does not show it, for the reason given there.
5. **Key rows** (nothing): the durations were right (0.68 us; 0.39 us for each step of ScalarE). Costing it at nothing in the changed kernel may stand, but by itself it gains 3.4 us (e6), since it shortens the row of VectorE that held groups 1 and 3 (9.8 to 6.3 us) and since the wait on issue was shorter there.
6. **The table** (nothing by itself): wrong for the kernel before: alone it gains 3.9 us (e4), and the piece of instructions that PE waited for starts ahead of the wait instead of 2.0 us into it. In the changed kernel its part is not shown. The stall (4.6 + 1.8 us in the sum) was a price that I kept as a constant and left to a rival, when the row beside it named a transfer; it was 3.3 and 1.8 us in the two profiles.
7. **The clock** (+2 for -3.2): the slow time stayed at about 5 us, where the sum had 3.8; PE's waits did not get shorter, 17.5 us in all for 14.4.

The profiled run is 12.5 us over the sum's 513.8: parts 3 and 4 have 8.2 of it (14.2 for 6), part 2 has 3.5, the clock 1.2, issue -1.3, and 0.9 have no place. So the late chunk is the largest single miss but not all of it: with pages in time, e1 still takes 519.0 us.

Of the rivals, the fourth named the mechanism (new waits in the old ones' place, "it needs weights that arrive late") and gave it 0.13 and 518.5 us; with its own bounds it could not reach 524.8. The first (the stall goes) came true in part in e14, 1.8 us. The third, a second stall, is not seen in the two profiles of the change, but e2 and e3 have the longer waits that it feared, with no more matmuls. Of the three signs of being wrong one came: PE still waits over 9 us in the stage, 17.5.

What stays open: 0.8 us of the ledger; what makes a piece of instructions start late in one variant and not in the next (2.9 us into the wait in e2, 1.6 us ahead of it in e14), beyond that the DMA engines are full wherever it does; and whether the early chunk saves time without such waits.

## What to carry to other kernels

When a queue issues in order and a change makes one of its requests earlier, list what comes behind it up to the event that it waits for: a prefetch asked for before its slot can be free delays everything else in the queue. Halving the columns of matmuls on a small tile doubles the instructions, and each half still takes 68% of the time of the whole; where they run in a row, look for waits on issue, hold them against the pieces of instructions in the view of the DMA queues, and keep large transfers away from them. Profile a kernel twice before a wait is explained: the same wait was 10.6 and 6.3 us here. And test the parts of a change one by one: here two of the four gain 5 us together (e11), and the whole change loses 6.6 (3.9 in e14).

## What the runs showed of the hardware

- 64 plain fp32 matmuls of 32x32 take 2.70 us with 256 columns and 1.83 us with 128, at 2.4 GHz: 42 and 29 ns each. The 1.83 us hold at DMA shares from 0.04 to 1.04 (the profile after).
- PE ran out of instructions: 28 waits on issue of 0.9 us or more in 16 profiles, each ending 1.2 to 1.7 us after a 16 KB piece of instructions had landed, which took 0.9 to 1.5 us. Where the piece started late, up to 3.3 us into the wait, the DMA share was 0.76 to 1.13, and the wait reached 6.1 us (e15).
- With 128 of the short matmuls in a row this happened 5 times, 15.7 us in all (e5); without most transfers 4 waits of 1.7 to 2.7 us were left (e13).
- The same 1 MB chunk landed 5.6 us after its issue before and 9.5 and 7.4 us in the two profiles of the change, and 10.1 us in e1, where nothing waited for it.
- The clock was granted at 1.2 GHz behind the waits of 5 us, in the changed kernel behind those of 10.6, 2.7 and 3.6 us; in e4 the issue wait of 1.8 us left the clock of its window at 1.00.
